# Sparse attention's queries rotated by pairs, its gates' weight third, mean squares spread over a projection, and the output sent in eight tiles

## The chip, the cores and the metric

The kernel runs on one core of a Trainium2 chip. The metric is the device time of one execution in microseconds, the median of three runs.

## The reference, cut to what matters

Two blocks of two layers each follow one another on 256 tokens of width 1024. The first block has a hybrid layer (a linear recurrence beside retention), a gated feed-forward, a sparse attention layer (NSA) and a second feed-forward. The second block has two layers with four branches, adaptive norms from a condition vector, and a gated merge. The change touches the sparse attention, the head norms of the second block's first layer, and the return of the result.

```python
def nsa(h, w_in, ...):
    proj = h @ w_in
    q = proj[..., :HD].reshape(B, S, H, dh)                 # 16 heads of 64
    k_cmp, v_cmp, k_slc, v_slc, k_win, v_win = ...          # 4 groups of 64 each
    gates = jax.nn.sigmoid(proj[..., HD + 6 * KV_WIDTH:].reshape(B, S, H, 3))
    q = rotary(q, pos, ROT_DIM, ROPE_THETA) * (dh ** -0.5)
    k_slc, k_win = rotary(k_slc, ...), rotary(k_win, ...)
    kc = rotary(compress(k_cmp, pe_k, k_w1, k_w2), cmp_end_np, ROT_DIM, ROPE_THETA)
    vc = compress(v_cmp, pe_v, v_w1, v_w2)                  # gelu(blocks @ w1) @ w2
    # per block of queries: softmax over kc, over selected blocks, over a window
    o = gb[..., 0:1] * o_cmp + gb[..., 1:2] * o_slc + gb[..., 2:3] * o_win
    return out @ w_out

def _modulation(cvec, w_ada, b_ada):
    m = jax.nn.silu(cvec) @ w_ada + b_ada

def _rms(x, w):                                             # also on each head of q and k
    return x * lax.rsqrt(jnp.mean(x * x, axis=-1, keepdims=True) + EPS) * w
```

## The kernel before, in words

Every engine has a program of its own, written out by hand in the order in which it is to work: `tensor`, `vector`, `scalar`, `gpsimd` and `sync`. Each engine counts its finished steps on one semaphore, and `pe.of(name)`, `ve.of(name)`, `ac.of(name)`, `gp.of(name)` give the count that a named step reaches.

**Weights.** The list `FLOW` has all weight chunks in order, each 128 x 2048 floats (1 MB, two DMAs of 512 KB on SyncE's queue). `load` (L220) brings a half chunk into one of four stage buffers. `high` (L226) has ScalarE write the rounded high part into WH, `low` (L233) has VectorE write the rest into WL. There are two WH/WL pairs, so the high part of a chunk waits until TensorE has finished the second chunk before it. `product` (L295) makes a matmul in three: high x high, high x low, low x high (L303 to L305; L300 to L302 with tokens as rows). `features` (L325) is eight such products into one tile of 128 outputs. `high_next` and `low_next` treat one chunk per call, so their places in each program fix what stands ahead of what.

**The sparse attention stage** (`nsa_tensor` L1418 and its four companions). TensorE multiplies, in this order, the chunk with the gates' weight (only 64 of its 256 columns a row are used), then kc, the turned gates (a transposition by an identity), vc, ks, kw, vs, the rotations of ks and kw, vw, and the four query chunks q0 to q3. A rotation (`rope_tensor` L462, `rope_vector` L470, `rope_gpsimd` L479) is a permuting matmul at L467, a multiplication by the sine on VectorE (L476), and a multiplication by the cosine and an addition on GpSimd (L485, L488). All eight query tiles are rotated after q3. Then come the compression's matmuls (L1468), which need all 32 block additions of VectorE (L1533), two gelus on ScalarE (L1636), the small matmuls kcT and vcs (L1476, L1480), and the rotation of the compressed keys. The first score waits for GpSimd to have rotated all of it.

**Attention** goes in 24 units. In turn n TensorE makes the scores of unit n + 1 (L1195, masks L1199), the values of unit n - 2 (L1512), one step of the modulation beside it, and turns the scaled scores of unit n - 1 (L1216). VectorE takes the maximum (L1238) and scales (L1257 to L1267), ScalarE takes the exponentials (L1307). Score n + 2 reuses the two PSUM banks of score n. The modulation (L1349) reads 24 weights of 1 MB through a ring of three slots (`ring_load` L274); the first two compression weights and a small third one go through the same ring ahead of them. Its input is the silu of the condition (L1375), after GpSimd has cleared the place for it (L1659). `due` shares 26 steps over 26 turns, so each turn has one.

**Mean squares of the heads** in the second block's first layer (`squares_tensor` L2038): 12 matmuls of two columns, each two passes (L2044, L2048), then the rotation of the raw heads. Two such blocks stand before and after the first of two outer projections (`outer_tensor` L2157), each of which has 48 matmuls of 512 columns. In the second layer they follow the values' tiles.

**The output** is one DMA of 1 MB (L2639) once VectorE has finished the last of eight result tiles (L2500).

## Time and profile before

| | |
|---|---|
| median of 3 runs | 1460.38 us (1460.25 to 1460.53) |
| profiled execution, its own time | 1460.34 us |
| its span | 1458.5 us |
| granted TensorE clock, mean | 0.991 |
| TensorE busy | 1414.2 us (97%) |
| VectorE busy | 843.6 us (58%) |
| ScalarE busy | 663.1 us (45%) |
| GpSimd busy | 156.2 us (11%) |
| DMA | 211.03 MB, 145 GB/s on the mean |

Times in the profile are from the start of the span. PE is TensorE's matmuls and PEld its weight loads, DVE is VectorE, ACT ScalarE, POOL GpSimd and SP SyncE. A matmul's duration covers its passage through the array; the distance from one start to the next tells how fast they follow. A clock of 1.00 is 2.4 GHz and 0.50 is 1.2 GHz. Idle time of an engine that is not the bottleneck costs nothing.

### The profile page before, as it was taken

The page shows a single profiled execution, that of the slowest core. Times are in us where ns is not written, and L with a number is a line of the kernel's source. Part 1 is how long each engine was busy: PE and PEld are TensorE (multiplying, and loading weights), DVE is VectorE, ACT ScalarE, POOL GpSimd, SP SyncE. Part 2 cuts the span into 40 slices and gives each one's busy share as a digit, 9 for nine tenths or more (in the row PEclk, how much of TensorE's full clock was granted, in tenths as well). Part 3 has the DMA queues.
Part 4 walks back from the last instruction along what each step waited for, and adds up shares of the span by engine and source line. Part 5 has one row for each costly group of instructions (what it writes and reads, how often), then busy time and mean ns, then how long its engine had stood idle before and what let it go on. Part 6 is the DMA issues. An engine that isn't in the chain of part 4 may idle for free.

```text
span 1458.5 us, 22837 instructions
## 1 busy us (share of the span) xinstructions
PE 1414.2 (97%) x9390; PEld 1212.6 (83%) x9390; DVE 843.6 (58%) x1295; ACT 663.1 (45%) x1159; POOL 156.2 (11%) x141
## 2 busy tenths in 40 slices
PE   9999999999899899999999999899999999999998
PEld 8989888889755688888888876788888889879998
DVE  6876788656546668885723347433323455674554
ACT  5645555444355555555442344423223345454442
POOL 0010111001300001110003000021111101101111
PEclk9999999999999999999999999999999999999999
DMA  8435655554477455555422210222322223313553
GB/s 310 138 117 174 225 182 193 192 189 151 170 287 263 152 178 189 188 189 174 145 87 78 86 59 1 87 87 88 114 88 88 99 103 116 134 46 130 199 177 115
DMA packets 56967, 211.03 MB, mean 145 GB/s; under 512 B 6176, under 2 KB 9888, under 8 KB 53536
## 3 DMA queue, kind: packets, MB, share of 16 engines
q1 hardware_dynamic: 56128, 206.40, 41.3%
q10 hardware_dynamic: 736, 3.18, 0.6%
q8 instruction: 74, 1.21, 0.3%
q14 instruction: 29, 0.24, 0.0%
HBM read 208.51 MB, written 1.05 MB: 144 GB/s over the span
## 4 chain that ended last, share of the span: by engine, by line
PE 90%; DVE 5%; ACT 2%; DMA 1%; issue 1%; POOL 1%; SPq 0%; ACTq 0%; DVEq 0%; POOLq 0%
PE psum L313 17%; PE psum L303 15%; PE psum L304 15%; PE psum L305 15%; PE psum L312 8%; PE psum L1195 2%; PE psum L1216 2%; PE psum L1349 2%; DVE WL L236 2%; PE psum L300 1%; PE psum L301 1%; PE psum L302 1%; PE psum L2398 1%; PE psum L1512 1%; PE psum L467 1%
## 5 line engine op out<-in xcount | busy, mean ns | idle before, releaser
L236 DVE TENSOR_TENSOR WL<-stage,WH 128x1024 fp32r<-128x1024 f32 x334 | 418.5, 1294 | 259.0 <-ACT WH L231 259.0
L231 ACT ACTIVATE WH<-stage 128x1024 fp32r<-128x1024 f32 x334 | 334.6, 1051 | 217.7 <-PE psum L305 162.6
L303 PE MATMUL psum<-XX,WH 128*128 128x256 f32 (+2 forms) x1208 | 392.6, 325 | 8.3 <-DVE WL L236 3.9
L304 PE MATMUL psum<-XX,WH 128*128 128x256 f32 (+2 forms) x1208 | 386.3, 320 | 0.0
L305 PE MATMUL psum<-XX,WL 128*128 128x256 f32 (+2 forms) x1208 | 385.9, 319 | 0.0
L313 PE MATMUL psum<-XX,WH 128*128 128x512 f32 x832 | 288.4, 397 | 0.0
L303 PEld LDWEIGHTS psum<-XX,WH 128*128 128x128 f32 (+1 forms) x1208 | 230.8, 191 | 35.4 <-issue 11.9
L304 PEld LDWEIGHTS psum<-XX,WH 128*128 128x128 f32 (+1 forms) x1208 | 231.1, 191 | 16.2 <-issue 0.5
L305 PEld LDWEIGHTS psum<-XX,WL 128*128 128x128 f32 (+1 forms) x1208 | 231.0, 191 | 16.1
L312 PE MATMUL psum<-XX,WL 128*128 128x256 f32 x728 | 203.4, 279 | 0.0
L313 PEld LDWEIGHTS psum<-XX,WH 128*128 128x128 f32 x832 | 150.2, 188 | 29.5 <-issue 1.2
L312 PEld LDWEIGHTS psum<-XX,WL 128*128 128x128 f32 x728 | 137.3, 189 | 5.0 <-DVE XX L406 0.3
L2567 POOL TENSOR_TENSOR arena<-arena,con 128x512 f32<-128x512 f32 (+1 forms) x48 | 51.5, 1072 | 400.2 <-DVE con L2485 399.6
L1307 ACT ACTIVATE arena<-psum,SM 128x16 f32<-128x16 f32 (+3 forms) x144 | 67.5, 479 | 25.9 <-DVE SM L1243 11.8
L313 PE MATMUL psum<-hidden,WH 128*128 128x512 f32 x224 | 78.6, 391 | 0.0
L1114 ACT ACTIVATE arena<-psum 128x512 f32<-128x512 f32 x44 | 26.3, 598 | 107.7 <-PE psum L313 107.7
L1292 ACT ACTIVATE arena<-psum 128x512 f32<-128x512 f32 (+2 forms) x48 | 35.4, 738 | 79.3 <-PE psum L1216 79.1
L312 PE MATMUL psum<-hidden,WL 128*128 128x256 f32 x224 | 63.1, 282 | 0.0
L2485 DVE TENSOR_TENSOR con<-psum,con 128x512 f32<-128x512 f32 (+1 forms) x48 | 26.2, 554 | 59.4 <-ACT con L2343 30.7
L2343 ACT ACTIVATE con<-psum,par 128x512 f32<-128x512 f32 (+1 forms) x64 | 35.6, 573 | 50.2 <-PE psum L305 50.2
L1238 DVE TENSOR_REDUCE SM<-psum 128x2 f32<-128x1024 f32 (+4 forms) x48 | 41.9, 873 | 25.7 <-PE psum L1199 15.6
L1155 POOL TENSOR_TENSOR arena<-arena,SM 128x512 f32<-128x512 f32 x22 | 30.1, 1366 | 201.9 <-ACT arena L1128 201.9
(285 smaller groups left out, 1979.0 us busy)
## 6 DMA issues: line engine op xcount, KB each, us to landing
stage<-w SPq DMA_DIRECT2D x132, 512.0 KB, 4.3
stage<-merge SPq DMA_DIRECT2D x80, 512.0 KB, 4.3
ring<-ada SPq DMA_DIRECT2D x24, 1024.0 KB, 4.8
stage<-in SPq DMA_DIRECT2D x44, 512.0 KB, 4.4
stage<-ab_in SPq DMA_DIRECT2D x24, 512.0 KB, 5.1
stage<-nsa_in SPq DMA_DIRECT2D x20, 512.0 KB, 4.6
stage<-out SPq DMA_DIRECT2D x16, 512.0 KB, 4.3
stage<-ab_out SPq DMA_DIRECT2D x8, 512.0 KB, 4.3
```

What stands on the lines that cost most here:

```text
L231: e.activation(hi, raw, ACT.Copy).then_inc(s_hi, 1)
L236: e.tensor_tensor(lo, raw, hi.bitcast(F32), ALU.subtract).then_inc(s_lo, 1)
L303: e.matmul(dst, wh, xh, start=start, stop=False)
L304: e.matmul(dst, wh, xl, start=False, stop=False)
L305: return e.matmul(dst, wl, xh, start=False, stop=stop)
L312: e.matmul(dst[:, 0:256], wl, x[:, 0, :], start=False, stop=False)
L313: t = e.matmul(dst[:, 0:512].rearrange("p (s n) -> p s n", s=2), wh, x, start=start, stop=stop)
L1238: e.tensor_reduce(nm, scored(p, n, u), AX.X, ALU.max, negate=True).then_inc(*ve.tick())
L1292: e.activation(dst, src, ACT.Copy).then_inc(*ac.tick(f"{p}.turned{n}"))
L1307: e.activation(s[:, q, h, :], v[:, q, h, :], ACT.Exp, bias=nm[:, q, h:h + 1], scale=rate, accum_out=sm[:, q, h:h + 1]).then_inc(*ac.tick(f ...
L2343: e.activation(L.SG[n % 2], banks[f"g{l}.{m}.{i}"][:, 0:L.NT], ACT.Sigmoid, bias=P("b_merge", l * 32 + MERGED[i] * 8 + m)).then_inc(*ac.ti ...
L2567: e.tensor_tensor(L.M[:, m, :], L.M[:, m, :], L.T2[n % 2], ALU.add).then_inc(*gp.tick(f"u{l}.{n}"))
```

## The change

Four edits. In the sparse stage the gates' weight goes third in `FLOW`, behind kc and vc, with the other programs following. The queries are rotated in four pairs: pair 0 after q1, pair 1 after q2, then the compression's matmuls, q3, pair 2, the small matmuls, and pair 3 after the compressed keys. VectorE makes the whole rotation of the compressed keys. Two steps of the modulation are taken ahead of the first score on every engine, and 24 steps are shared over the 26 turns, which leaves turns 0 and 13 with none; clearing and silu of the condition move into the first feed-forward part. In the second block's first layer, both blocks of mean squares are made inside the first outer projection, two matmuls ahead of each of its products. The output is sent in eight DMAs, one for each result tile.

```diff
-                FLOW += [("nsa_gates", 0)] + [("nsa_in", c) for c in (4, 5, 6, 8, 7, 9, 0, 1, 2, 3)]
+                FLOW += [("nsa_in", 4), ("nsa_in", 5), ("nsa_gates", 0)] + [("nsa_in", c) for c in (6, 8, 7, 9, 0, 1, 2, 3)]
@@ ffn_scalar, after the masks
+                    e.wait_ge(*gp.of("m.zero"))
+                    e.activation(M.c[:, :, 0:2], P("cvec", 0, 16).rearrange("p (k v) -> p k v", v=2), ACT.Silu).then_inc(
+                        *ac.tick("m.c"))
@@ ffn_gpsimd, after rms_gpsimd
+            if l == 0:
+                e.wait_ge(*ve.of("h.end"))
+                e.wait_ge(*gp.now())
+                e.memset(M.c, 0.0).then_inc(*gp.tick("m.zero"))
@@ nsa_tensor
+            fm(4, "n.kc")
+            fm(5, "n.vc")
             w = Chunk(flow, "nsa_gates", 0)
...
-            fm(4, "n.kc")
+            fm(6, "n.ks")
             b = tile(e, "n.turned.gates")
...
-            for c in range(4):
-                fm(c, f"n.q{c}")
-            e.wait_ge(*ve.of("n.q3"))
-            rope_tensor(e, "nq", N.q, 8, C("p8"))
+            def rope(c):
+                e.wait_ge(*ve.of(f"n.q{c}"))
+                rope_tensor(e, f"nq{c}", N.q[:, 2 * c:2 * c + 2, :], 2, C("p8"))
+
+            fm(0, "n.q0")
+            fm(1, "n.q1")
+            rope(0)
+            fm(2, "n.q2")
+            rope(1)
...
+            fm(3, "n.q3")
+            rope(2)
...
             rope_tensor(e, "nkc", N.kcT[:, :, 0:15], 2, C("p8"), n=15)
-            pe.mark("n.ready")
+            rope(3)
+            beside = modulation_tensor(e, rings)
+            for _ in range(2):
+                next(beside)
...
-                    e.wait_ge(*gp.of("nkc.roped"))
+                    e.wait_ge(*ve.of("nkc.roped"))
+                    e.wait_ge(*gp.of("nkw.roped"))
                     e.wait_ge(*ac.of("masks"))
+                if br == 0 and it == 0:
+                    e.wait_ge(*gp.of(f"nq{2 * t2 + f}.roped"))
...
-            attend_tensor(e, "n", N.units, N.S, N.T, scores, values, modulation_tensor(e, rings), 26)
+            attend_tensor(e, "n", N.units, N.S, N.T, scores, values, beside, 24)
@@ nsa_vector
             some(9)
+
+            def rope(c):
+                rope_vector(e, f"nq{c}", N.tmp[:, 2 * c:2 * c + 2, :], 2, C("nsin"))
+
+            e.wait_ge(*gp.of("nkw.roped"))
+            rope(0)
             low_next(e, flow)
             scaled(e, N.q[:, 4:6, :], "n.q2", "nn")
+            rope(1)
             scaled(e, N.q[:, 6:8, :], "n.q3", "nn")
-            e.wait_ge(*gp.of("nkw.roped"))
-            rope_vector(e, "nq", N.tmp, 8, C("nsin"))
...
+            rope(2)
             rope_vector(e, "nkc", N.kct[:, :, 0:15], 2, C("esin"), n=15)
+            kc = N.kcT[:, :, 0:15]
+            e.tensor_tensor(kc, kc, spread(C("ecos"), 2, 15), ALU.mult).then_inc(*ve.tick())
+            e.wait_ge(*ve.now())
+            e.tensor_tensor(kc, kc, N.kct[:, :, 0:15], ALU.add).then_inc(*ve.tick("nkc.roped"))
+            rope(3)
@@ nsa_gpsimd
-            rope_gpsimd(e, "nq", N.q, N.tmp, 8, C("ncos"))
-            rope_gpsimd(e, "nkc", N.kcT[:, :, 0:15], N.kct[:, :, 0:15], 2, C("ecos"), n=15)
-            e.wait_ge(*ve.of("h.end"))
-            e.wait_ge(*gp.now())
-            e.memset(M.c, 0.0).then_inc(*gp.tick("m.zero"))
+            for c in range(4):
+                rope_gpsimd(e, f"nq{c}", N.q[:, 2 * c:2 * c + 2, :], N.tmp[:, 2 * c:2 * c + 2, :], 2, C("ncos"))
@@ keys_tensor, layer 0
-                squares_tensor(e, L, 0)
-                outer_tensor(e, flow, L, *OUTER[0])
-                squares_tensor(e, L, 1)
+                outer_tensor(e, flow, L, *OUTER[0], [squares_tensor(e, L, br) for br in range(2)])
@@ squares_tensor, now a generator
+            tiles = [(2 * n, 2, n) for n in range(4)] + [(8 + 4 * n + 2 * a, a, n) for n in range(L.nt) for a in range(2)]
+            for i, (c, a, n) in enumerate(tiles):
+                t = e.matmul(b[:, c:c + 2], S3[:, a, n * 128:(n + 1) * 128], C("bones2"), start=True, stop=True)
+                if i + 1 == len(tiles):
+                    t.then_inc(*pe.tick(f"{p}.var"))
+                if i % 2:
+                    yield
             e.wait_ge(*ac.of(f"{p}.raw"))
             rope_tensor(e, p, L.R[br][:, :, 0:256], 3, C("p16"))
+            yield
@@ outer_tensor
+                def x(k):
+                    if l == 1 and r + a == 0:
+                        e.wait_ge(*ve.of(f"n{l}0.x{k}"))
+                    if beside:
+                        next(beside[a], None)
+
                 features(e, b[:, 0:NT], w, a * 128, f"l{l}.o{r}{a}", x, L.xs())
+                if beside:
+                    run(beside[a])
@@ sync
-            e.wait_ge(*ve.of("l1.end"))
-            e.dma_start(out.rearrange("p (k n) -> p k n", k=8), X[:, :, NOW]).then_inc(s_out, 16)
-            e.wait_ge(s_out, 16)
+            y = out.rearrange("p (k n) -> p k n", k=8)
+            for m in range(8):
+                e.wait_ge(*ve.of(f"o1.{m}.0"))
+                e.dma_start(y[:, m, :], X[:, m, NOW]).then_inc(s_out, 16)
+            e.wait_ge(s_out, 8 * 16)
```

VectorE and ScalarE in the sparse stage follow the new order of chunks: the copy of the gates' products comes after n.vc is scaled, and `inverse_scalar` comes after two `high_next` calls instead of three. `modulation_scalar` loses the silu, `nsa_vector` and `nsa_scalar` take two steps of `beside` ahead of their 24 too, and `finish` loses its wait for the rotated queries.

## Rows read from the trace of the kernel before

**Rows 1.** The page, busy time of an engine, share of the span, instructions.
```profile
PE 1414.2 (97%) x9390; PEld 1212.6 (83%) x9390; DVE 843.6 (58%) x1295; ACT 663.1 (45%) x1159; POOL 156.2 (11%) x141
```

**Rows 2.** TensorE's waits, 300 to 410 us: total, times, longest.
```profile
PE psum L1195 <- POOL arena L488: 4.0, 1, 4.0
PE psum L303 <- DVE WL L236: 2.0, 1, 2.0
PE psum L1349 <- DVE SM L1263: 1.5, 1, 1.5
PE psum L467 <- DVE arena L419: 0.8, 1, 0.8
PE psum L1476 <- ACT arena L1636: 0.4, 1, 0.4
```

**Rows 3.** Windows: length, busy (instructions) by engine, clock, DMA share, GB/s.
```profile
320.00:323.30 3.30, 3.30 (x18) 3.30 (x18) 2.67 (x4) 0.52 (x1) 0.00 (x0) 0.51 0.87 278
...
330.00:352.00 22.00, 22.00 (x186) 22.00 (x185) 13.48 (x19) 8.37 (x11) 0.45 (x4) 1.00 0.50 167
```

**Rows 4.** Timeline where TensorE passes from one chunk to the next.
```profile
346.41 0.28 PE L300 MATMUL psum<-WH,XX 128*128 128x256 f32 x1
...
347.76 2.36 DVE L236 TENSOR_TENSOR WL<-stage,WH 128x1024 fp32r<-128x1024 f32 x2 [1.87 <-ACT WH L231]
```

**Rows 5.** Windows over the first turns of the sparse attention.
```profile
397.00:402.00 5.00, 3.49 (x24) 2.90 (x28) 1.95 (x8) 3.00 (x11) 0.18 (x1) 0.50 0.47 198
402.00:410.00 8.00, 8.00 (x82) 4.43 (x74) 3.11 (x10) 4.39 (x18) 0.00 (x0) 0.80 0.62 235
```

**Rows 6.** Timelines of TensorE and ScalarE, the first turns of the sparse attention.
```profile
398.31 1.23 PE L1195 MATMUL psum<-arena 64*128 64x128 f32 x8
...
409.96 0.71 PE L1195 MATMUL psum<-arena 64*128 64x128 f32 x8
...
411.04 0.65 PE L1512 MATMUL psum<-arena 128*64 128x256 f32 x4
...
399.87 0.21 ACT L1307 ACTIVATION_READ_ACCUMULATOR arena<-psum,SM 128x1 f32 x1
...
401.40 0.23 ACT L1375 ACTIVATE con<-par 128x16 f32<-128x16 f32 x1
```

**Rows 7.** Block additions, the high part behind n.q1, landing of the compression's weight.
```profile
375.50 3.03 DVE L1533 TENSOR_TENSOR arena<-arena 64x120 f32<-64x120 f32 x9
...
371.41 2.01 ACT L231 ACTIVATE WH<-stage 128x1024 fp32r<-128x1024 f32 x2 [3.75 <-PE psum L305]
...
ring<-cmp_v SPq DMA_DIRECT2D x1, 512.0 KB, 8.7
```

**Rows 8.** The second block of mean squares; windows behind the first.
```profile
779.51 0.95 PE L2044 MATMUL psum<-con,arena 128*128 128x2 f32 x8
...
782.11 1.54 PE L467 MATMUL psum<-arena,con 128*128 128x512 f32 x4
...
761.00:767.00 6.00, 6.00 (x32) 4.71 (x31) 0.90 (x3) 3.06 (x4) 2.18 (x2) 0.71 0.00 0
767.00:773.00 6.00, 6.00 (x21) 4.75 (x20) 4.60 (x5) 0.00 (x0) 5.43 (x5) 0.72 0.37 126
```

**Rows 9.** Small matmuls of a norm between two products.
```profile
1188.85 0.94 PE L362 MATMUL psum<-con,SM 128*128 128x1 f32 x8
1189.65 0.36 PE L303 MATMUL psum<-early,WH 128*128 128x258 f32 x1
```

**Rows 10.** DMAs with median us to landing; window of the output; the ring's issues.
```profile
out<-X SPq DMA_DIRECT2D x1, 1024.0 KB, 4.8
...
arena<-pe ACTq DMA_DIRECT2D x2, 16.0 KB, 2.2
...
1455.00:1456.00 1.00, 0.00 (x0) 0.00 (x0) 0.00 (x0) 0.00 (x0) 0.00 (x0) 1.00 1.01 350
...
389.35 88.27 SPq L279 DMA_DIRECT2D ring<-ada x24
```

More of the change, by code:

```diff
@@ L1373, in modulation_scalar @@
         def modulation_scalar(e):
-            e.wait_ge(*gp.of("m.zero"))
-            e.activation(M.c[:, :, 0:2], P("cvec", 0, 16).rearrange("p (k v) -> p k v", v=2), ACT.Silu).then_inc(
-                *ac.tick("m.c"))
             for c in range(25):
@@ L1424, in fm @@
                 for h in range(2):
-                    features(e, b[:, h * 256:(h + 1) * 256], w, h * 128, name, None, CTX)
+                    x = (lambda k: e.wait_ge(*ve.of(f"nn.x{k}"))) if name == "n.kc" and h == 0 else None
+                    features(e, b[:, h * 256:(h + 1) * 256], w, h * 128, name, x, CTX)
                     next(rms, None)
@@ L1449, in nsa_tensor @@
             i.then_inc(*pe.tick("n.turned.gates"))
-            fm(5, "n.vc")
-            fm(6, "n.ks")
             fm(8, "n.kw")
@@ L1543, in nsa_vector @@
             low_next(e, flow)
-            e.wait_ge(*pe.of("n.gates"))
-            e.tensor_copy(N.tmp[0:64, 0, :], banks["n.gates"][0:64, 0:256]).then_inc(*ve.tick("n.gates"))
-            banks.emptied("n.gates", ve)
-            low_next(e, flow)
             next(rms)
@@ L1553, in nsa_vector @@
             scaled(e, N.vc, "n.vc", "nn")
+            e.wait_ge(*pe.of("n.gates"))
+            e.tensor_copy(N.tmp[0:64, 0, :], banks["n.gates"][0:64, 0:256]).then_inc(*ve.tick("n.gates"))
+            banks.emptied("n.gates", ve)
+            low_next(e, flow)
             low_next(e, flow)
@@ L1589, in nsa_vector @@
             banks.emptied("n.vcs", ve)
+            rope(2)
             rope_vector(e, "nkc", N.kct[:, :, 0:15], 2, C("esin"), n=15)
+            kc = N.kcT[:, :, 0:15]
[3 more added lines that the diff above has]
+            rope(3)
             e.wait_ge(*ac.of("n.gates"))
+            beside = modulation_vector(e)
+            for _ in range(2):
+                next(beside)
             def finish(n):
@@ L1604, in finish @@
                 banks.emptied(f"n.value{it}{t2}{f}", ve)
-            attend_vector(e, "n", N.units, N.S, N.T, finish, modulation_vector(e), 26, True)
+            attend_vector(e, "n", N.units, N.S, N.T, finish, beside, 24, True)
             parts_low(e, ve, "n", N.att, (1, 3, 5, 7))
@@ L1614, in nsa_scalar @@
             e.dma_start(N.pe2[64:128, :], A["pe"]).then_inc(s_pe2, 16)
+            for _ in range(2):
+                high_next(e, flow)
+            inverse_scalar(e, "nn")
             for _ in range(3):
                 high_next(e, flow)
-            inverse_scalar(e, "nn")
-            high_next(e, flow)
             e.wait_ge(*pe.of("n.turned.gates"))
@@ L1623, in nsa_scalar @@
             banks.emptied("n.turned.gates", ac)
-            for c in range(2):
-                high_next(e, flow)
+            high_next(e, flow)
             e.wait_ge(*pe.of("n.vs"))
@@ L1637, in nsa_scalar @@
                 banks.emptied(name, ac)
-            attend_scalar(e, "n", N.units, N.S, N.T, modulation_scalar(e), 26, True)
+            beside = modulation_scalar(e)
+            for _ in range(2):
+                next(beside)
+            attend_scalar(e, "n", N.units, N.S, N.T, beside, 24, True)
             def ready(k):
@@ L2002, in all_keys_tensor @@
                     w.done()
-                squares_tensor(e, L, j)
+                run(squares_tensor(e, L, j))
         def context_keys_tensor(e, flow, L, norm):
@@ L2155, in keys_gpsimd, with outer_tensor @@
             e.tensor_tensor(L.rs[br][:, 8:z], L.ms[br][:, 8:z], C("mhalf", 0, z - 8), ALU.pow).then_inc(*gp.tick(f"{p}.qpow"))
-        def outer_tensor(e, flow, L, c, r):
+        def outer_tensor(e, flow, L, c, r, beside=None):
             l, NT = L.l, L.NT
```

11 lines of the change are left out of this document (removed).

## The prediction

> **What bounds the kernel now.** I read the page's busy times first, then TensorE's waits, then the granted clock by stretches, and last the timelines around the four places that the diff touches. TensorE is busy 97% of the span [rows 1], so nothing is won by making another engine faster; time can only come out of TensorE's idle time (some 44 us in all), out of stretches in which its clock is at 1.2 instead of 2.4 GHz, and out of the tail after its last matmul. The change adds and removes no matmul. So I price it as idle time plus clock loss plus tail, before and after.
>
> In the list of waits the reader is to see that five of TensorE's waits between 300 and 410 us, 8.7 us together, lie where the sparse attention stage is reordered [rows 2]. The windows show what the list does not: after two of these waits the clock is granted at half. Where the window says 0.51, 18 matmuls start in 3.3 us; at full clock 186 start in 22 us, 0.118 each [rows 3].
>
> **Gates third.** The gates' weight is as long a transfer and conversion as any chunk, but only 64 columns are used: 24 matmuls, 24 x 0.118 = 2.8 us, where a chunk gives 48 x 0.118 = 5.7 us. Standing first, it ends before the next chunk's low half is there: 2.0 us of wait [rows 2]. The half clock behind it costs 3.3 - 18 x 0.118 = 1.2 us [rows 3]. With n.kc first, the same conversion (done near 319) has until 314 + 5.7 = 319.7, so both go. What is late next? The chunk behind the gates, n.ks, can only be converted once the second chunk before it is done, n.vc. The handover of a full chunk [rows 4]: the matmul after a chunk's last one starts at 346.41; the next but one chunk's low part starts at 347.76, 2.36 us for its two halves, so the first half is ready at 348.9, 2.5 us after the chunk's end. The gates cover 2.8 us, a margin of 0.3. If the margin is gone, it costs a few tenths: I take 0, with 0.5 as the other end. The four DMAs that change place on SP's queue are all 512 KB. The gain is 3.2 us (2.0 to 3.7).
>
> **Queries rotated by pairs, and what is pulled into the hole.** Before, GpSimd rotates all eight query tiles and then the compressed keys, and TensorE waits 4.0 us for the last of it; it also waits 0.8 for n.q3, 0.4 for the gelu, and 1.5 before the first modulation matmul, which is put down to a DVE row but ends when ACT has the silu of the condition (401.40 + 0.23), which stood behind the first exponentials and between two table loads [rows 2, 6]. Sum 6.7 us. The clock is 0.50 over 3.49 us of matmul time and 0.80 over 8.00 us: 1.7 + 1.6 = 3.3 us lost [rows 5]; not all of that work runs with the clock, I take 3.0.
>
> After the change, following TensorE in order (small durations without a row are those of the same operations in this stretch's timeline): the first pair's rotation follows n.q1, the second n.q2. Then the compression matmuls, which wait for the 32 block additions on DVE. Those end at 375.50 + 3.03 = 378.5; TensorE gets there at 371.4 (n.q1 done, when ACT starts the next high part) + 0.9 + 5.7 + 0.9 = 378.9 [rows 7]. It just fits; below, 0.5 us. Their weights are issued at 370 and land 8.7 us later at the latest [rows 7], 378.7, before the second of the two is reached. Moving them ahead of n.q3 puts the gelus behind 5.7 us of matmuls, and frees the first ring slots some 8 us earlier. Then n.q3, the third rotation, kcT, vcs, the keys' rotation, the fourth, and two modulation steps of 1.0 each before the first score. The vector engine needs from n.q3's end 0.7 (scale) + 0.2 + 0.4 (copies) + 0.7 (sine of pair 2) + 3 x 0.2 (keys' rotation, two of these operations new to it) with gaps about 3.7 us; TensorE needs 0.9 + 0.3 + 0.6 + 0.2 + 0.9 + 2.0 = 4.9 us. So the first score doesn't wait. GpSimd's last pair is done some 6 us after n.q3, and is first read nine units later, so the new waits of the scores on it cost nothing; without that distance one of its operations, 1.3 us, would show.
>
> What comes back: turn 0 has no modulation step left (24 steps over 26 turns leave turns 0 and 13 empty). Score 2 needs the banks of score 0, free when its exponentials are: 399.87 + 0.21 - 398.31 = 1.8 us after score 0, of which score 1 fills 1.1 (411.04 - 409.96) [rows 6]: 0.7 us of wait. Turn 13 has its scaled scores early: 0.3, at most the step's own 1.0. Small waits between kcT and the fourth rotation: 0.2. The gain is 6.7 + 3.0 - 1.2 = 8.5 us. The ends: 5, if the block additions, the first score and turn 13 each wait a microsecond more, and 10, if no wait is left. ACT also loses two table loads here, and the silu with GpSimd's memset moves into the first feed-forward part, where both have room; uncovered it would be 0.3 us.
>
> **Mean squares spread.** Each of the two blocks is 24 passes of matmuls with two columns. The second takes 782.11 - 779.51 = 2.6 us [rows 8]. After the first the clock falls: 6.0 us at 0.71 and 6.0 at 0.72 lose 1.7 + 1.7 = 3.4 us, though TensorE never idles there [rows 8]. Spread, every group of four passes stands between three matmuls of 512 columns. The nearest row for that is the mean of a norm between two products: eight passes take 0.80 (1188.85 to 1189.65) [rows 9], 0.1 each, the same as in the block; entering and leaving a group hides one weight load and shows another, and the next product is about 0.1 longer. Six groups: 6 x 0.5 = 3.0 us against 2.6, so +0.4 for each block, +0.1 for its rotation in the midst of products: +0.9 us for both. The clock loss, taken as 3.2, goes if no stretch is left that is nearly all small matmuls; I take that, since TensorE kept the full clock in the second block, which is split by nothing, and in stretches that mix small pieces with full ones. Net gain 2.3 us. The other end is a clock at half through all of the first outer projection. DVE and GpSimd get the first variances some 4 us later and the second ones some 4 earlier; both chains have the projections of 11 us each before them. Without that cover 3 us would show.
>
> The Trainium skill (TensorE: Matmul & The Clock Gate, Why this matters for your kernels) asks to avoid long idle gaps between bursts because they bring the clock down. The trace agrees in rows 2 and 3, but rows 8 show a fall without a gap. By that rule alone the spread would return nothing and the sum would be 3.2 us higher.
>
> **Output by tiles.** The last transfer now is 1 MB, 4.8 us from issue to landing, with 350 GB/s at its height, so 3.0 us of data and 1.8 of the rest [rows 10]. The last tile is 128 KB: 1.8 + 0.4 = 2.2 us, and 16 KB rows land in 2.2 [rows 10]. Seven tiles leave while TensorE makes the next, one per 2.8 us. Gain 2.6 us, ends 2.0 and 2.8. The Trainium skill (DMA: Bandwidth & Descriptors, Rules for kernel authors) advises at least 1 MiB per DMA for bandwidth, which speaks against the split. By that page's fixed cost of about 2 us the last tile would take an estimated 2.4 us, and the sum would move by 0.2.
>
> **Sum.** The profiled execution took 1460.34 us with a span of 1458.5; the median of the three runs is 1460.38, so the two are the same for this purpose. 1460.3 - 3.2 - 8.5 - 2.3 - 2.6 = 1443.7 us.
>
> **Rivals.**
> (a) The clock stays low in the spread squares. For it: rows 8 show that small matmuls without idle time bring it down, and now there are two blocks of them in a row. Against: each group stands beside 0.7 us of full-width work. If the loss only stays, +3.2: 1446.9. If both halves, some 17 us, run at half, 8.5 lost instead of 3.2: 1443.7 + 8.5 = 1452.
> (b) A new wait replaces part of the hole: TensorE reaches the compression, the first modulation step or the first score before DVE or the ring is ready, and the clock dips again. For it: margins of 0.3 us twice. Against: the order above has each input ready first. Half of the 8.5 returned gives 1448.
> (c) The modulation weights become the bound, and the kernel is slower. Before, three of the 24 loads of 1 MB land while TensorE stands in the hole; after, it asks for them sooner and one turn earlier. The 24 are issued over 88.27 us, one per turn of 3.7 on the mean; a load alone takes 3.0 at 350 GB/s [rows 10]. Each microsecond over is paid up to 24 times; it decides when a load takes 0.8 us longer than a turn, 4.5 us: 24 x 0.8 = 19 us, 1443.7 + 19 = 1463. Against: 3.0 is far from 4.5, and no wait of TensorE is put down to a transfer in this stage before.
> (d) The waits only move: shared conversion of weights limits the stage anyway, and the time stays within 0.2%, about 1460. Against: behind the hole no wait for weights is listed in this stage.
>
> **How the numbers follow.** Forecast 0.72, by itself 1441 to 1447; (a) 0.12; (b) 0.10; (c) 0.03; (d) 0.03. The fall of the clock near the end of the sparse attention, unchanged work behind which some 1.7 us are lost, may go or double. Range 1440.5 to 1449.0: it takes in (b) and the milder (a). A measurement of this kernel tells about 0.2%, 2.9 us, from no change. Faster 0.94, same 0.03, slower 0.03.
>
> **What would show it.** TensorE's list of waits has no 4.0 on GpSimd, no 2.0 on WL at the start of the sparse stage, and a wait of some 0.7 us at score 2. The windows over the gates, the first turns and the first outer projection all read 1.00. The last DMA lands 2.2 us after issue. It is wrong if WL, the block additions or a ring slot stand in TensorE's waits for over 1 us, or if a window in the first outer projection reads below 0.9.

## The result and the profile after

The changed kernel takes 1443.12 us (median of 4 executions, 1442.77 to 1443.66), the kernel before 1460.32 (4 executions, 1459.46 to 1460.53). The ratio is 0.9884 with a 95% interval of 0.9867 to 0.9901: faster by 1.2%, some 17 us. The profiled execution took 1443.66 us with a span of 1441.9, 16.7 us less than the profiled execution of before; the prediction's sum was 16.6. The mean granted clock rose from 0.991 to 0.999. The sum is right to a tenth, but its terms are not, and the next sections are about that.

The page's busy times of the changed kernel. TensorE has the same 9390 matmuls as in [rows 1], and 7.4 us less busy time; the same instructions can be shorter by the clock and by passes that overlap otherwise.

```profile
PE 1406.8 (98%) x9390; PEld 1205.8 (84%) x9390; DVE 848.0 (59%) x1297; ACT 660.6 (46%) x1157; POOL 157.5 (11%) x139
```

TensorE's waits between 300 and 410 us, the counterpart of [rows 2]. Five waits of 8.7 us together have become three of 2.6.

```profile
PE psum L1202 <- ACT arena L1314: 1.4, 1, 1.4
PE psum L1477 <- DVE arena L1550: 0.8, 1, 0.8
PE psum L1356 <- DVE MOD L1370: 0.4, 1, 0.4
```

Windows of the changed kernel: the start of the sparse stage, its first turns, and the first outer projection (length, busy time and instructions by engine, clock, DMA share, GB/s). They answer to [rows 3, 5, 8].

```profile
318.00:324.00 6.00, 6.00 (x54) 6.00 (x51) 3.90 (x7) 2.44 (x3) 1.98 (x6) 1.00 0.53 166
...
394.00:397.00 3.00, 3.00 (x28) 1.40 (x27) 2.37 (x8) 1.10 (x7) 0.00 (x0) 0.63 0.78 330
397.00:400.00 3.00, 3.00 (x30) 1.84 (x32) 0.62 (x4) 1.96 (x9) 0.00 (x0) 0.80 0.64 205
...
750.00:756.00 6.00, 6.00 (x38) 5.26 (x38) 0.00 (x0) 3.07 (x4) 0.00 (x0) 1.00 0.00 0
756.00:762.00 6.00, 6.00 (x33) 4.82 (x32) 3.37 (x6) 0.60 (x1) 4.25 (x3) 1.00 0.01 3
762.00:768.00 6.00, 6.00 (x35) 5.07 (x35) 2.42 (x2) 0.00 (x0) 5.57 (x4) 1.00 0.51 175
```

The gates' stretch and the outer projection have the full clock. The first turns don't: 3 x 0.37 + 3 x 0.20 = 1.7 us are lost, behind the one wait of over 1 us that is left.

Timelines of the changed kernel, the rows on which the account below rests: the first matmul of n.vs, the compression, the first scores, the last product of the sparse attention, and the first group of mean squares with the rotation behind its six groups.

```profile
342.66 0.28 PE L300 MATMUL psum<-WH,XX 128*128 128x256 f32 x1
...
375.78 3.91 PE L1477 MATMUL psum<-arena,ring 128*64 128x60 f32 x64 [0.76 <-DVE arena L1550]
...
485.18 1.08 PE L1529 MATMUL psum<-arena 128*64 128x256 f32 x8 [0.87 <-DVE arena L1296]
...
750.95 0.51 PE L2072 MATMUL psum<-con,arena 128*128 128x2 f32 x4
752.10 0.50 PE L2072 MATMUL psum<-con,arena 128*128 128x2 f32 x4
...
757.82 1.45 PE L467 MATMUL psum<-arena,con 128*128 128x512 f32 x4
```

The tail of the changed kernel: SyncE's wait for its last transfer, and VectorE's last instruction. In the kernel before the same two rows are below it.

```profile
SPq L2691 <- DMA out<-X: 1.5, 1, 1.5
...
1439.06 0.48 DVE L2537 SCALAR_TENSOR_TENSOR X<-psum,MOD,X 128x256 f32<-128x256 f32 x1 [2.31 <-PE psum L305]
```

```profile
SPq L2652 <- DMA out<-X: 4.2, 1, 4.2
...
1452.84 0.48 DVE L2500 SCALAR_TENSOR_TENSOR X<-psum,MOD,X 128x256 f32<-128x256 f32 x1 [2.32 <-PE psum L305]
```

An account follows from instructions that both traces have. How much earlier each comes in the changed kernel, and what each step of it adds:

| point, before and after | earlier by | this stretch | term predicted |
|---|---|---|---|
| start of the sparse stage, 314.23 and 314.02 | 0.2 | 0.2 | |
| n.vs's first matmul, 346.41 and 342.66 | 3.75 | 3.5 | 3.2 |
| last product of the sparse attention, 494.65 and 485.18 | 9.47 | 5.7 | 8.5 |
| first mean squares, 761.32 and 750.95 | 10.37 | 0.9 | 0 |
| a norm's small matmuls, 1188.85 and 1175.43 | 13.42 | 3.05 | 2.3 |
| VectorE's last instruction, 1452.84 and 1439.06 | 13.78 | 0.4 | |
| end of the span, 1458.5 and 1441.9 | 16.7 | 2.9 | 2.6 |

The last row goes by the executions' own times, 1460.34 and 1443.66; the spans are rounded. The fourth stretch holds no change at all. Its 0.9 us is the dip behind the end of the sparse attention, which this execution doesn't have. So the rotation's term fell short by 2.8 us, and smaller gains elsewhere plus the absent dip made it good.

### The profile page after: what moved, and what is told of

The parts are those of the page before. It is cut to its first block, busy times and chain, and to the rows that moved or that the text cites. A ratio compares the mean times of both kernels' runs of the same rounds, so it can differ in the third digit from the quotient of the medians.

```text
span 1441.9 us, 22843 instructions
## 1 busy us (share of the span) xinstructions
PE 1406.8 (98%) x9390; PEld 1205.8 (84%) x9390; DVE 848.0 (59%) x1297; ACT 660.6 (46%) x1157; POOL 157.5 (11%) x139
## 4 chain that ended last, share of the span: by engine, by line
PE 90%; DVE 5%; ACT 2%; DMA 1%; issue 1%; POOL 0%; SPq 0%; DVEq 0%; ACTq 0%
PE psum L313 17%; PE psum L303 15%; PE psum L304 15%; PE psum L305 15%; PE psum L312 8%; PE psum L1202 2%; PE psum L1223 2%; PE psum L1356 2%; DVE WL L236 2%; PE psum L300 1%; PE psum L301 1%; PE psum L302 1%; PE psum L2435 1%; PE psum L1529 1%; PE psum L467 1%
## 5 line engine op out<-in xcount | busy, mean ns | idle before, releaser
L236 DVE TENSOR_TENSOR WL<-stage,WH 128x1024 fp32r<-128x1024 f32 x334 | 421.4, 1303 | 253.3 <-ACT WH L231 253.3
L303 PE MATMUL psum<-XX,WH 128*128 128x256 f32 (+1 forms) x1208 | 392.4, 325 | 6.1 <-issue 1.8
L304 PE MATMUL psum<-XX,WH 128*128 128x256 f32 (+1 forms) x1208 | 384.3, 318 | 0.0
L305 PE MATMUL psum<-XX,WL 128*128 128x256 f32 (+1 forms) x1208 | 384.2, 318 | 0.0
L303 PEld LDWEIGHTS psum<-XX,WH 128*128 128x128 f32 x1208 | 229.0, 190 | 32.7 <-issue 9.5
L305 PEld LDWEIGHTS psum<-XX,WL 128*128 128x128 f32 x1208 | 229.1, 190 | 16.1
L304 PEld LDWEIGHTS psum<-XX,WH 128*128 128x128 f32 x1208 | 229.2, 190 | 15.7 <-issue 0.7
L313 PEld LDWEIGHTS psum<-XX,WH 128*128 128x128 f32 x832 | 150.2, 188 | 29.5 <-issue 1.2
L312 PEld LDWEIGHTS psum<-XX,WL 128*128 128x128 f32 x728 | 137.3, 189 | 4.9 <-DVE XX L406 0.3
L1245 DVE TENSOR_REDUCE SM<-psum 128x2 f32<-128x1024 f32 (+4 forms) x48 | 41.9, 873 | 18.4 <-PE psum L1202 10.2
```

The costliest lines, as they stand in the source:

```text
L236: e.tensor_tensor(lo, raw, hi.bitcast(F32), ALU.subtract).then_inc(s_lo, 1)
L303: e.matmul(dst, wh, xh, start=start, stop=False)
L304: e.matmul(dst, wh, xl, start=False, stop=False)
L305: return e.matmul(dst, wl, xh, start=False, stop=stop)
L312: e.matmul(dst[:, 0:256], wl, x[:, 0, :], start=False, stop=False)
L313: t = e.matmul(dst[:, 0:512].rearrange("p (s n) -> p s n", s=2), wh, x, start=start, stop=stop)
```

## The experiments

### Each part by itself

Four kernels, each the kernel before with one part of the change. Their edits are those of the diff shown ahead: the output's last hunk, the hunks of `keys_tensor`, `squares_tensor` and `outer_tensor`, the new place in `FLOW` with the programs that follow it, and all the rest of the sparse stage.

> The kernel before with the output sent tile by tile, nothing else. The prediction's term is -2.6 us (2.0 to 2.8): the last transfer becomes 128 KB, and SyncE's last wait on it falls from 4.2 us to about 1.5. The rival is that the seven earlier transfers disturb TensorE's last stage or that landing costs the same whatever the size: then less than 1 us is gained.

> The kernel before with the spread mean squares of the queries' and keys' heads, nothing else. The prediction: -2.3 us, made of a clock loss of 3.2 returned (the two windows behind the first block read 1.00 instead of 0.71 and 0.72) and 0.9 of added cost (three groups by about 0.46 and a later rotation). The rival: the dip behind the block has to do with its distance from the earlier stage, not with the block, so that it comes back elsewhere in the outer projections and the time rises by 0.9 us.

> The kernel before with the sparse gates' weight third, nothing else. The prediction: -3.2 us (2.0 to 3.7), the 2.0 wait on WL gone and the window behind it at 1.00; the trace of the changed kernel has 3.55 between the same two points. The rival: the gain is paid back at the hole of some 4 us ahead of the first scores, because GpSimd's rotation and the shared conversion don't get earlier by as much as TensorE does: then less than 2 us is left.

> The kernel before with the queries rotated by pairs and everything that is pulled ahead with it (two modulation steps, the silu, the compression's place), nothing else. The prediction's term is -8.5 us (5 to 10). The trace of the changed kernel has 5.7 to 5.9 between the gates and the last sparse product, plus 0.9 to 1.7 from a dip at 497 to 501 that is gone. If the parts are independent this run gives -6.5 to -7.5; if the dip at 497 stays when the earlier stages are not moved, -5.8.

All on one chip (9, 11, 12 and 5 executions), beside 27 executions of the kernel before (median 1460.0):

| part alone | median us | ratio, 95% | gain from the ratio, us | predicted |
|---|---|---|---|---|
| output by tiles | 1456.13 | 0.9973 (0.9963 to 0.9982) | 3.9 (2.6 to 5.4) | 2.6 |
| squares spread | 1457.58 | 0.9985 (0.9976 to 0.9993) | 2.2 (1.0 to 3.5) | 2.3 |
| gates third | 1457.04 | 0.9982 (0.9972 to 0.9992) | 2.6 (1.2 to 4.1) | 3.2 |
| rotation by pairs, with what is pulled ahead | 1451.21 | 0.9943 (0.9930 to 0.9956) | 8.3 (6.4 to 10.2) | 8.5 |

The four gains sum to 17.0 us, the gain of the whole; with intervals this wide that says only that the parts don't disturb each other by more than some 4 us. The rivals of the first two expectations are outside the intervals. That of the third, less than 2 us left, is not, and the trace decides: 3.75 us ahead of before at n.vs's first matmul and 3.9 at the last product of the sparse attention, so nothing is paid back in between. The rotation's 8.3 us lies above both figures that were expected, and its interval excludes only the 5.8. Each interval is over 2 us wide, and the reason is more than noise. The profile of the kernel with the new output alone shows why. Windows of it, at a place that this kernel has in common with the kernel before:

```profile
318.00:324.00 6.00, 5.36 (x51) 4.67 (x52) 4.65 (x6) 2.08 (x3) 0.00 (x0) 1.00 0.61 179
760.00:766.00 6.00, 6.00 (x26) 4.59 (x26) 1.70 (x5) 2.55 (x4) 3.00 (x3) 0.62 0.00 0
```

Its list of waits has the same `PE psum L303 <- DVE WL L236` of 2.0 us as [rows 2], and here no dip follows it: 1.00 where [rows 3] has 0.51. The other dips are there, as at 760. So that profiled execution was 2.0 us ahead at the end of the sparse attention (492.65 for 494.65) through nothing in its edit. Of the 45 executions of the kernel before in the three sets of runs here, 35 take 1458.8 to 1461.8 us at a mean clock of 0.991 or 0.992, and 10 take 1454.8 to 1456.9 at 0.993 to 0.995. Whether a dip comes differs from one execution to the next.

How often it comes, and what it costs, can be read by comparing traces, those of the runs further down too, over a stretch in which they do the same work:

| same stretch | us without a dip | us with one |
|---|---|---|
| start of the sparse stage to n.vs's first matmul, with the 2.0 us wait | 30.7 in 3 traces | 32.2 (before) |
| n.vs's first matmul to the last product of the sparse attention, all with the waits of 0.76 and 1.39 at the compression and score 2 | 141.0 (the changed kernel, run once more) | 142.5 to 142.6 in 3 (changed, rotation alone, squares in blocks) |
| last product of the sparse attention to the first mean squares | 265.8 in 5 | 266.6 to 267.1 in 8 |
| first mean squares to a norm's small matmuls, squares in blocks | 424.2 in 2 (gates alone, rotation alone) | 427.5 to 427.6 in 3 (before, output alone, squares in blocks) |
| the same, squares spread | 424.4 to 424.5 in 8 | none |

So the dip at the start of the sparse stage and the one behind score 2 cost 1.5 us each where they come, the one behind the sparse attention 0.8 to 1.3, and the one (or the two) at the blocks of mean squares 3.3. The profile of before has a dip at the first, third and fourth of these places, and one behind the 4.0 us of waiting ahead of the first scores; this last one is in all four traces that have that wait. The prediction left open the one behind the sparse attention and counted the others as certain. The last two rows also give the price of the spread by itself, against blocks that keep their clock: 0.2 to 0.3 us. Windows over the first block, with the gates third alone and with the rotation alone:

```profile
757.00:763.00 6.00, 6.00 (x39) 5.08 (x38) 2.14 (x5) 3.06 (x4) 2.47 (x2) 1.00 0.00 0
...
753.00:759.00 6.00, 6.00 (x38) 5.09 (x37) 1.86 (x5) 3.06 (x4) 2.19 (x2) 1.00 0.00 0
```

The clock's part of a term is therefore an expected value, and one trace shows one draw of it. The output's 3.9 us is a case in point: the tail's own rows give 2.9 (table above), its list of waits has the 1.5 us on the last transfer for 4.2, and the rest lies outside its edit; draws of the dips can make it, though no run separates them.

The kernel with the rotation alone has its last product of the sparse attention at 487.88, 6.8 us ahead of before. It has no dip at 320 either, and stands 1.1 us ahead at n.vs's first matmul (345.35 for 346.41); the other 5.7 is what the changed kernel has in the same stretch. Its waits behind the gates' stretch are the three of the changed kernel. It also shows where the 0.4 us of the last but one row in the account comes from: of the four parts alone, only this one has it. Why is open. In the traces of the other two the edits do what they should: with the gates third the 2.0 us on WL is gone; with the squares spread the windows from 756 to 780 all read 1.00.

### Do small matmuls in a block bring the clock down?

```diff
-                outer_tensor(e, flow, L, *OUTER[0], [squares_tensor(e, L, br) for br in range(2)])
+                squares_tensor(e, L, 0)
+                outer_tensor(e, flow, L, *OUTER[0])
+                squares_tensor(e, L, 1)
```

> The changed kernel with the mean squares of the queries' and keys' heads in two undivided blocks of 24 small passes again, nothing else. If the block brings the clock down, the windows behind the first block read 0.7 again and the time is 2.3 us (by the trace 2.7) above the changed kernel: about 1445.6. The rival, by which the dip came from where the first block happened to lie: no dip, and the time falls by the 0.9 us that the spread costs, to 1442.2.

Measured: 1446.42 us (6 executions, ratio 0.9915, 0.9898 to 0.9931). The changed kernel has 1443.12 on one chip and 1443.97 on another: 2.5 to 3.3 us less. Timeline of this kernel at the two blocks, and windows behind them:

```profile
750.73 0.95 PE L2073 MATMUL psum<-con,arena 128*128 128x2 f32 x8
751.54 2.19 PE L2077 MATMUL psum<-con,arena 128*128 128x2 f32 x16
753.59 2.91 PE L467 MATMUL psum<-arena,con 128*128 128x512 f32 x4
...
767.32 0.95 PE L2073 MATMUL psum<-con,arena 128*128 128x2 f32 x8
768.13 1.93 PE L2077 MATMUL psum<-con,arena 128*128 128x2 f32 x16
769.92 2.73 PE L467 MATMUL psum<-arena,con 128*128 128x512 f32 x4
```

```profile
750.00:756.00 6.00, 6.00 (x33) 4.72 (x32) 0.57 (x3) 3.06 (x4) 1.85 (x2) 0.75 0.00 0
756.00:762.00 6.00, 6.00 (x27) 4.92 (x26) 4.93 (x5) 0.00 (x0) 5.43 (x5) 0.96 0.34 107
...
768.00:774.00 6.00, 6.00 (x32) 4.79 (x32) 4.53 (x8) 2.01 (x3) 2.25 (x2) 0.72 0.38 128
```

The block starts 0.2 us from where the first group of the changed kernel stands, and 10.6 us earlier than in the kernel before, and the dip is there all the same. The rival by which the dip came from where the block lay falls. But the block doesn't bring it each time: behind the first block it is in 3 of the 5 traces of kernels with undivided blocks (table above), and in none of 8 with the squares spread. Here the second block brings a dip as well, which it didn't in [rows 8], while one of the six executions, 1443.26 us at a mean clock of 0.999, has hardly any. So the second block's full clock, on which the prediction leaned, was a draw and not a property of that block.

### What holds the first turns back

The trace of the changed kernel has the cause next to the wait. Timelines of it, around the first two scores: TensorE, VectorE and GpSimd.

```profile
393.75 0.71 PE L1202 MATMUL psum<-arena 64*128 64x128 f32 x8 [1.39 <-ACT arena L1314]
...
388.54 1.18 DVE L1617 TENSOR_TENSOR arena<-arena 128x30 f32<-128x30 f32 x1
389.64 0.68 DVE L476 TENSOR_TENSOR arena<-psum,con 128x512 f32<-128x512 f32 x1
391.39 0.22 DVE L1245 TENSOR_REDUCE SM<-psum 128x4 f32<-128x64 f32 x1 [1.07 <-PE psum L1206]
391.65 0.88 DVE L1248 TENSOR_SCALAR SM<-SM 128x4 f32<-128x4 f32 x1
392.44 0.68 DVE L1245 TENSOR_REDUCE SM<-psum 128x4 f32<-128x512 f32 x1
393.16 0.17 DVE L1248 TENSOR_SCALAR SM<-SM 128x4 f32<-128x4 f32 x1
...
388.40 1.28 POOL L488 TENSOR_TENSOR arena<-arena 128x512 f32<-128x512 f32 x1 [0.56 <-DVE arena L476]
389.82 1.27 POOL L485 TENSOR_TENSOR arena<-arena,con 128x512 f32<-128x512 f32 x1
391.24 1.27 POOL L488 TENSOR_TENSOR arena<-arena 128x512 f32<-128x512 f32 x1
```

VectorE's scaling of four maxima takes 0.88 us at 391.65 and 0.17 at 393.16. The long one ends at 392.53, and GpSimd's addition, under way since 391.24, ends at 392.51. The last addition for the keys, 30 columns in 1.18 us, ends at 389.72, and the GpSimd operation beside it at 389.68. Both read SBUF and start inside a GpSimd operation, and both last until that is over. The operation at 389.64 has one input in PSUM; GpSimd starts on its next operation at 389.82 and neither is longer than elsewhere. The first exponentials wait for 391.65's result, and score 2 for them: 0.7 of the 1.39 us. The Trainium skill (SBUF — State Buffer, Who interferes with whom) describes this as an exclusive lock on ports that the two engines share, taken by whichever comes first for the whole instruction, for VectorE operations with two SBUF inputs (388.54) and some with one (391.65 is of the kind named), not for one that has its only other input in PSUM (389.64). The trace agrees in these three places. The test was to move GpSimd's work away:

```diff
             for c in range(4):
+                if c == 3:
+                    e.wait_ge(*ve.of("n.max1"))
                 rope_gpsimd(e, f"nq{c}", N.q[:, 2 * c:2 * c + 2, :], N.tmp[:, 2 * c:2 * c + 2, :], 2, C("ncos"))
```

> The changed kernel with GpSimd's rotation of the last query pair begun only when the second score's maximum is taken, nothing else. If DVE's small reductions are slow (0.88 and 1.18 us for 0.17) because GpSimd works beside them, the wait at score 2 falls from 1.39 to about the 0.7 that was predicted, and the dip behind it may shorten: 0.7 to 2 us less than the changed kernel. If DVE is slow there for another reason, no change in the wait. GpSimd's last product would then be done near 396, ahead of its first reader nine scores later.

Measured: 1443.36 us (5 executions, ratio 0.9899, 0.9880 to 0.9917), no change from the changed kernel. But the wait did what was expected. Timelines of this kernel, VectorE, GpSimd and TensorE:

```profile
391.66 0.17 DVE L1248 TENSOR_SCALAR SM<-SM 128x4 f32<-128x4 f32 x1
...
393.42 1.26 DVE L1267 TENSOR_TENSOR SM<-SM,arena 128x4 f32<-128x4 f32 x1
...
394.98 1.17 DVE L1274 TENSOR_TENSOR arena<-arena,SM 128x64 f32<-128x64 f32 x1
...
393.39 1.28 POOL L485 TENSOR_TENSOR arena<-arena,con 128x512 f32<-128x512 f32 x1 [3.70 <-DVE SM L1264]
...
394.81 1.26 POOL L488 TENSOR_TENSOR arena<-arena 128x512 f32<-128x512 f32 x1
...
393.05 0.71 PE L1202 MATMUL psum<-arena 64*128 64x128 f32 x8 [0.68 <-ACT arena L1314]
...
396.31 0.60 PE L1223 MATMUL psum<-con,arena 128*16 128x128 f32 x4 [1.10 <-DVE arena L1274]
```

The scaling of the maxima is back to 0.17 us and the wait at score 2 is 0.68, the prediction's 0.7. GpSimd's two operations now meet two others of VectorE's, which last until 394.68 and 396.15 (GpSimd's end at 394.67 and 396.07), and TensorE waits 1.10 us for the second. The collision moved with GpSimd's work, and that shows its cause; it didn't go away.

The other way is to give TensorE something for that gap. First by spreading 26 steps instead of 24:

```diff
-            attend_tensor(e, "n", N.units, N.S, N.T, scores, values, beside, 24)
+            attend_tensor(e, "n", N.units, N.S, N.T, scores, values, beside, 26)
```

(and the same number for `attend_vector` and `attend_scalar`.)

> The changed kernel with 26 modulation steps laid over the 26 turns, so that turns 0 and 13 have one each where they had none, nothing else; the number of steps up to the end stays 24, two of them ahead, so the last two turns have none. If the 1.39 us wait at score 2 is what brings the dip at 394 to 398, both go: 1.4 + 1.7 = about 3 us less than the changed kernel, 1440. If ACT has no room for the exponential and the step's silu side in turn 0, the wait only moves: 1443. If the dip has another cause, 1.4 less: 1441.7.

Measured: 1443.93 us (4 executions, ratio 0.9899, 0.9881 to 0.9917), no change from the changed kernel. TensorE's waits in this kernel from 410 to 495 us:

```profile
PE psum L1223 <- DVE arena L1274: 2.0, 2, 1.6
```

The changed kernel has 0.5 us on the same TensorE line there. The turns at the end, which lost their steps, now wait for VectorE (at 479.24 and 482.72). At score 2 the wait fell from 1.39 to 0.39 us. What was won in turn 0 is spent at the end, and 0.4 us more is put down to the DMA of a modulation weight, which TensorE now wants one step earlier. The dip at 394 is absent here, but it is absent in the changed kernel run again too, with its wait of 1.39 us, so this trace doesn't tell whether the shorter wait took it away.

### Two versions that are faster

The block additions: VectorE makes the low part of the last query weight ahead of them, though TensorE wants it only at 379.6.

```diff
             some(6)
-            low_next(e, flow)
             scaled(e, N.q[:, 2:4, :], "n.q1", "nn")
             some(9)
+            low_next(e, flow)
```

> The changed kernel with DVE's last nine block additions and the scaling of the second query pair ahead of the low part of the last query weight (3.28 us of DVE work that is needed only at 379.6), nothing else. The compression's wait of 0.76 us on the additions goes, and the additions end near 372.4 instead of 375.6: about 0.8 us less than the changed kernel. The rival: the stage buffer comes free 3 us later, and the loads of the modulation weights behind it arrive later: a wait on WH or WL of 1 us or more appears near 385, and the time rises by about that.

Measured: 1442.25 us (4 executions, ratio 0.9891, 0.9872 to 0.9910), 0.9 to 1.7 below the changed kernel on the two other chips, which the interval alone doesn't settle. The trace does: no wait at the compression, and no new one on WH, WL or the ring. Timelines of VectorE, first the changed kernel, then this one, with GpSimd's row ahead:

```profile
368.74 3.28 DVE L236 TENSOR_TENSOR WL<-stage,WH 128x1024 fp32r<-128x1024 f32 x2 [0.47 <-ACT WH L231]
371.94 0.68 DVE L419 TENSOR_TENSOR arena<-psum,SM 128x512 f32<-128x512 f32 x1
372.65 2.98 DVE L1550 TENSOR_TENSOR arena<-arena 64x120 f32<-64x120 f32 x9
```

```profile
368.51 1.31 POOL L485 TENSOR_TENSOR arena<-arena,con 128x512 f32<-128x512 f32 x1 [10.20 <-PE psum L467]
...
369.03 3.59 DVE L1550 TENSOR_TENSOR arena<-arena 64x120 f32<-64x120 f32 x9
372.65 2.36 DVE L236 TENSOR_TENSOR WL<-stage,WH 128x1024 fp32r<-128x1024 f32 x2
```

The low part takes 3.28 us beside GpSimd's product for the first pair (368.50, 1.30 us) and 2.36 us alone; the additions, when they are the ones beside it, take 3.59 for 2.98. It is the same collision. The windows of this trace read 1.00 from 392 to 404, though its list of waits still has the 1.4 us at score 2: another wait without a dip. From n.vs's first matmul to the last product of the sparse attention it takes 140.2 us, the changed kernel run again, also without a dip there, 141.0: the expected 0.8.

Last, one modulation step ahead of the first score and one in turn 0:

```diff
-            return range((n + 1) * steps // (N + 2) - n * steps // (N + 2))
+            return range((n + 1) * steps // (N + 2) - n * steps // (N + 2) + (p == "n" and n == 0))
...
-            for _ in range(2):
+            for _ in range(1):
                 next(beside)
```

> The changed kernel once more, as it is, as the measure for the other two on the same chip: 1443.1 by its first four executions. By all theories 1442 to 1444; where executions differ, by dips of the clock that come in some and not in others, 1 to 2 us each.

> The changed kernel with one modulation step ahead of the first score instead of two, and the other one in turn 0, which had none; all later turns as they were. The wait at score 2 falls from 1.39 us to 0.4, as in the run with 26 steps, and no turn at the end goes bare. DVE's rotation of the compressed keys then ends 0.3 us after TensorE wants its first score, so 0.3 comes back: 0.7 us less than the changed kernel by the waits, up to 2 us less where the dip at 394 goes with them. If the keys' rotation is later than that, the two cancel: no change.

> The same, with DVE's last nine block additions and the scaling of the second query pair also ahead of the low part of the last query weight. If the two add up: 0.7 to 0.8 us less than the run with one step ahead, 1.5 us less than the changed kernel by the waits (about 1441.6), and up to 3 less where the clock stays full through the stage. If the additions' wait was hiding work of GpSimd or ACT, a new wait takes its place at the first score: less than 0.5 of it shows.

On one chip, beside 7 executions of the kernel before (median 1459.53):

| kernel | median us | all | ratio, 95% | n.vs's first matmul to the last product, sparse attention |
|---|---|---|---|---|
| changed kernel again | 1443.97 | 1443.46 to 1444.83 | 0.9898 (0.9883 to 0.9912) | 141.0 |
| one step ahead | 1441.93 | 1441.69 to 1442.63 | 0.9883 (0.9866 to 0.9899) | 140.0 |
| and additions first | 1441.49 | 1440.75 to 1442.23 | 0.9880 (0.9865 to 0.9895) | 139.2 |

TensorE's waits of the kernel with one step ahead, from 300 to 410 us; the last kernel has the same list without its first line:

```profile
PE psum L1477 <- DVE arena L1550: 0.8, 1, 0.8
PE psum L1356 <- DVE MOD L1370: 0.4, 1, 0.4
PE psum L1202 <- DVE arena L1617: 0.2, 1, 0.2
```

The 1.4 us at score 2 is gone entirely, not down to 0.4: the scaling of the maxima now starts at 391.75, 0.15 us ahead of GpSimd's addition at 391.90, and takes 0.17. The keys' rotation still ends late behind GpSimd (L1617, 1.17 us) and costs 0.2. The whole of the executions of one step ahead lies below those of the changed kernel: 2.0 us by the medians, of which the stretch in the table shows 1.0. What the other 1.0 is, no run tells. Additions first takes another 0.8 us from the stretch, its own wait again, and 0.4 from the medians, whose executions overlap. The last kernel has the lowest median here, 2.5 us below the changed one.

## Why the prediction was right, and where it wasn't

**What bounds the kernel.** Right: the whole gain is idle time, clock and tail of TensorE. No other engine's busy time mattered, and VectorE's rose by 4.4 us. What was wrong is that the dips of one profile were taken as certain.

**Gates third.** Right in its mechanism and as a whole size: 3.5 us between the same two points, for 3.2. The 0.3 us of margin at n.ks held. Its clock term, taken as 1.2 us and worth 1.5, is in 1 of 4 traces with that wait; without it the edit is worth 2.0 (30.7 to 28.6 us for the stretch). Alone the part gave 2.6 us (1.2 to 4.1).

**Queries by pairs.** Right that all of the 6.7 us of waits goes. The steps that failed are three small ones, two of them with one cause. "It just fits; below, 0.5 us", of the compression: 0.76 us of wait, since the low part of a weight ahead of the additions took 3.28 us instead of 2.36. "0.7 us of wait", at score 2: 1.39. And "I take 3.0", of the clock returned: the dip behind that wait in the profiled execution costs 1.5 us again. The prediction's sign that the windows over the first turns read 1.00 failed there (0.63 and 0.80). Against these stand 0.5 us of small costs for turn 13 and between kcT and the fourth rotation, of which 0.4 us came, in another place. 0.76 + 0.7 + 1.5 - 0.1 = 2.9 us for a shortfall of 2.8. The changed kernel run again confirms the sum: without the dip the stretch falls short by 1.3 us (148.2 - 141.0 = 7.2 for 8.5), and 0.76 + 0.7 - 0.1 is 1.4. The cause of the first two: each duration was taken from a row in which VectorE worked beside an idle GpSimd. Before, GpSimd rotated between 384.8 and 397, while VectorE had almost nothing to do, so no row of that stretch shows them together. Spreading GpSimd's work over the chunks put it beside VectorE's conversions, additions and small reductions, each of which then lasts until GpSimd's operation has ended, or the other way round. The two runs that moved GpSimd's or VectorE's work show it. The third is the draw of an execution: the changed kernel run again has full clock in those turns with the same wait, and a dip at 488 instead.

**Mean squares spread.** Right, with a size off: 3.05 us for 2.3. The spread costs 0.2 to 0.3 us for both blocks by the table of stretches, where 0.9 was taken: a group of four passes shifts the products from 0.68 to 1.15 us apart, 2.8 for six, where 3.0 was taken. The clock gave 3.3 back. But this is the gain over an execution with the dip. Where the blocks keep their clock, as in 2 of 5 traces, the spread loses its 0.2 to 0.3, and the 2.2 us that the part gave alone is a mean over both kinds. The rule of the Trainium skill (TensorE: Matmul & The Clock Gate, Why this matters for your kernels) on idle gaps, by which the spread would return nothing, was weighed against [rows 8] and given up for them; the run with blocks bears the rows out, since the dip came back without any idle time of TensorE.

**Output by tiles.** Right: 2.9 us in the tail for 2.6, a tenth past the upper end. The profile has 2.0 us in the median from issue to landing of a tile, for 2.2.

**The dip at the end of the sparse attention**, "may go or double": gone in the profiled execution, worth 0.9 us. It is at 488 in the changed kernel run again.

**The rivals.** (a) didn't occur: all windows over the spread squares read 1.00, in eight traces. (b) is what happened in small: a third of the hole's gain was replaced by new waits and a dip behind them; its price of 4.3 us was too high. (c) did not occur, no wait is put down to the modulation weights in the changed kernel; wanted one step earlier still, they cost 0.4 us once. (d) did not occur.

So the sum is right to 0.1 us in the profiled execution, and to 0.6 in the medians, because 2.8 us too much in one term met 0.3 + 0.75 + 0.3 too little in the three others, 0.9 us from a dip that stayed away, and 0.6 between the points. That the terms cancel so closely is luck. It is luck too that the profile of before had a dip in all four places: the profiles of the parts alone each lack one or more with which their edit has nothing to do. The range from 1440.5 to 1449.0 had room for either.

## What to carry to other kernels

When work is moved from a stretch in which its engine was alone to one in which GpSimd and VectorE both read SBUF, allow for up to the other engine's operation, here 1.3 us and in the cases seen 0.6 to 1.1, on top of any VectorE duration on the critical path, however short it is in the trace; then order the two so that they take turns. A wait of over a microsecond on a TensorE that is otherwise full, or some 24 tiny passes in a row, can be followed by a stretch at half clock: here behind the 2.0 us wait in 1 of 4 traces, behind the 1.4 us wait in 3 of 5, behind the block in 3 of 5. Price it with what it costs times how often it comes, and compare kernels over several executions; where two traces must do, compare them stretch by stretch, between points that both have, with the windows of the clock beside it. A filler step is best taken from a turn with a surplus: 26 steps over 26 turns moved the gap to the end, and one step moved from ahead of the first score into turn 0 closed it.

## What the runs showed that was not expected

- VectorE's operations on 128x4 elements (L1248, L1267) took 0.88 and 1.26 us for 0.17, ending within 0.02 us of a GpSimd operation that had started before it; in the other direction GpSimd's addition of 1.29 us took 2.18 at 376.44, beside the conversions of a weight.
- The clock's dips are draws. The same 2.0 us wait was followed by a clock of 0.51 in one trace and 1.00 in three others, and the kernel before falls into executions of 1454.8 to 1456.9 us (10 of 45) and of 1458.8 to 1461.8 (35 of 45). What decides between them stays open. The two groups lie some 4 us apart. If the faster one is that in which the dip at the blocks of mean squares stays away, which no trace of it tells, the spread is worth an estimated 35/45 x 3.3 - 0.3 = 2.3 us; measured alone it gave 2.2.
- Over the 6 us with and behind a block of 24 matmul passes of two columns the clock was 0.62 to 0.75 without any idle time of TensorE, at two different distances from the stages before, but in 3 of 5 traces only; behind the same passes in groups of four between wide products it never fell, in 8 traces. With the blocks' dip the kernel loses 3.3 us, without it the blocks are 0.2 to 0.3 us cheaper than the spread.
